# Moving the first two softmax heads ahead of v's eviction, and splitting that eviction between two engines, in a two-layer streaming encoder

## What is computed

```python
def even_mixer(h, P, ...):
    xa, ga, q, k, v = split(h @ w_in0)
    ya = rglru(xa, gates)[h] * gelu(ga)              # the recurrence
    s  = q @ k.T * DHB ** -0.5 + rel_bias            # 8 heads of 64
    yb = softmax(s) @ v
    return concat(ya, yb) @ w_out0
mod = silu(c) @ w_mod[l] + b_mod[l]                  # 1024 x 6144, for each layer
```

## Time and profile before

| | us |
|---|---|
| median of 3 runs | 1857.21 (1856.42 to 1857.47) |
| the profiled execution's own time | 1840.97 |
| its span, first to last instruction | 1839.2 |
| PE busy | 1715.2 (93%) |
| DVE busy | 860.9 (47%) |
| ACT busy | 278.8 (15%) |
| mean granted PE clock | 0.943 of full |

### The profile page before, as it was taken

One profiled execution on the slowest core, in us unless ns is written; L12 is line 12 of the kernel. 1 busy time (PEld: TensorE's weight loads), 2 busy tenths in 40 slices (PEclk: granted clock), 3 DMA queues, 4 the chain that ended last, 5 costly groups with the idle time before them and its releaser, 6 DMA issues.

```text
span 1839.2 us, 25633 instructions
## 1 busy us (share of the span) xinstructions
PE 1715.2 (93%) x9272; PEld 982.1 (53%) x9272; DVE 860.9 (47%) x2514; ACT 278.8 (15%) x643; POOL 112.7 (6%) x115
## 2 busy tenths in 40 slices
PE   5999998999999999998999888879999999999996
PEld 2663466544444444345776788756544444444443
DVE  3205424455555455445662654334455555555445
ACT  2132412100011001003112122102101100010001
POOL 0000000100000000000000232100100000000000
PEclk9997869999999999998999799679999999999998
DMA  9966833879999999995331000014779999999993
GB/s 384 333 257 240 318 140 138 316 325 420 419 420 418 409 419 420 419 420 203 115 137 69 0 1 1 3 72 183 280 312 420 419 420 414 406 421 419 419 421 136
DMA packets 81235, 528.08 MB, mean 287 GB/s; under 512 B 13104, under 2 KB 13632, under 8 KB 20400
## 3 DMA queue, kind: packets, MB, share of 16 engines
q1 hardware_dynamic: 68256, 496.14, 66.4%
q0 software_dynamic: 9024, 20.03, 2.9%
q10 hardware_dynamic: 3824, 10.20, 1.6%
HBM read 533.04 MB, written 5.86 MB: 293 GB/s over the span
## 4 chain that ended last, share of the span: by engine, by line
PE 82%; DMA 10%; DVE 5%; issue 2%; ACT 1%; SPq 0%; POOL 0%; ACTq 0%; DVEq 0%; POOLq 0%
PE ps L662 20%; PE ps L462 14%; PE ps L706 11%; PE ps L689 10%; DMA arena<-in_wexp 4%; DMA ring<-in_wexp 4%; PE ps L425 3%; PE ps L646 3%; DVE arena L1247 2%; PE ps L434 2%; PE ps L609 1%; PE ps L909 1%; PE ps L912 1%; PE ps L442 1%; PE ps L531 1%
## 5 line engine op out<-in xcount | busy, mean ns | idle before, releaser
L1253 DVE SCALAR_TENSOR_TENSOR x<-ps,mod,x 128x256 f32<-128x256 f32 (+1 forms) x1024 | 329.1, 363 | 188.8 <-PE ps L706 119.0
L662 PE MATMUL ps<-arena 128*32 128x512 f32 (+2 forms) x1456 | 308.0, 606 | 8.2 <-DMA arena<-in_wexp 8.2
L706 PE MATMUL ps<-arena 128*128 128x288 f32 x960 | 264.9, 417 | 6.4 <-DVE x L1253 4.3
L706 PEld LDWEIGHTS ps<-arena 128*128 128x128 f32 x960 | 172.2, 189 | 139.3 <-issue 94.2
L662 PE MATMUL ps<-ring,arena 128*64 128x512 f32 (+1 forms) x976 | 211.4, 597 | 1.2 <-DMA arena<-in_wexp 1.2
L462 PE MATMUL ps<-h,ring 128*128 128x288 f32 x768 | 193.6, 414 | 2.1 <-ACT h L1009 2.1
L662 PEld LDWEIGHTS ps<-arena 128*32 128x32 f32 (+2 forms) x1456 | 92.4, 128 | 149.6 <-issue 149.1
L462 PEld LDWEIGHTS ps<-h,ring 128*128 128x128 f32 x768 | 148.3, 194 | 43.8 <-issue 3.0
L1247 DVE TENSOR_TENSOR arena<-ps,arena 128x256 f32<-128x256 f32 (+6 forms) x153 | 56.1, 373 | 213.2 <-issue 170.2
L689 PE MATMUL ps<-ring,arena 128*64 128x512 f32 (+2 forms) x624 | 135.5, 628 | 11.1 <-DMA ring<-in_wexp 11.1
L1561 DVE COPY arena<-ps 128x512 f32<-128x512 f32 x60 | 41.5, 691 | 174.0 <-PE ps L689 168.9
(11 more groups left out here) (270 smaller groups left out, 1670.0 us busy)
## 6 DMA issues: line engine op xcount, KB each, us to landing
arena<-in_wexp SPq DMA_DIRECT2D x210, 1024.0 KB, 23.3
ring<-in_wexp SPq DMA_DIRECT2D x180, 1024.0 KB, 23.0
ring<-in_wmod SPq DMA_DIRECT2D x48, 1024.0 KB, 7.3
ring<-in_win SPq DMA_DIRECT2D x26, 1024.0 KB, 5.1
ring<-in_wout SPq DMA_DIRECT2D x8, 1024.0 KB, 4.9
h_rows<-arena ACTq DMA_DIRECT2D x4, 512.0 KB, 2.6
x<-in_x ACTq DMA_DIRECT2D x1, 1152.0 KB, 16.3
out_y<-h SPq DMA_DIRECT2D x2, 576.0 KB, 2.8
```

The costliest lines, as they stand in the source:

```text
L662: last = mm(ps[2][w, :], xgT[:, r % 2, 4 * q + k, w], unit(("gu", l, s0 + i, q))[:, k * 512:(k + 1) * 512], start=(q == 0 and k == 0), sto ...
L706: mm(ps[ADD_BANKS[c]][:, 0:T], yb[:, r % 2, c * 128:(c + 1) * 128], onehot[:, r % 2, :], start=True, stop=True).then_inc(sem["add_ps"], 1)
L1253: return V.scalar_tensor_tensor(out=o, in0=a, scalar=s, in1=b, op0=op0, op1=op1)
```

## The change

The maxima of heads 0 and 1, the exponential of both, and the normalisation of head 0 now stand ahead of v's eviction. ACT evicts v's first tile (new semaphore `v_ev0`) and DVE the other two. PE's wait for v moves behind the scores of head 2 and the transpose of head 0. ACT's three stores of v stand where the exponential of head 1 stood. The closing steps of the recurrence are spread behind the normalisations of heads 0, 2 and 3 (`finish`). No instruction is added or dropped but the waits, and one copy changes its engine.

PE:

```diff
-            pe.wait_ge(sem["v_ev"], 1)
             for n, (j, hd) in enumerate(units):
...
                 last.then_inc(sem["pt_ps"], 1)
+                if n == 0:
+                    pe.wait_ge(sem["v_ev0"], 1)
+                    pe.wait_ge(sem["v_ev"], 1)
```

ACT:

```diff
             softmax_exp(0)
+            softmax_exp(1)
+            act.wait_ge(sem["v_ps"], 2)
+            A(vtm[:, 0, :], ps[4][:, :], ACT.Copy).then_inc(sem["v_ev0"], 1)
             for b in range(MOD_AHEAD // 2):
                 mod_rows(1, b, 3)
-            act.wait_ge(sem["v_ev"], 1)
-            for j, (t0, P) in enumerate(TILES):
-                act.dma_start(t["v"][t0:t0 + P, :], vtm[0:P, j, :]).then_inc(sem["st_mix"], 16)
             for n in range(24):
...
-                if n + 1 < 24:
-                    softmax_exp(n + 1)
+                if n:
+                    if n + 1 < 24:
+                        softmax_exp(n + 1)
+                else:
+                    act.wait_ge(sem["v_ev0"], 1)
+                    act.wait_ge(sem["v_ev"], 1)
+                    for i, (i0, R) in enumerate(TILES):
+                        act.dma_start(t["v"][i0:i0 + R, :], vtm[0:R, i, :]).then_inc(sem["st_mix"], 16)
```

DVE:

```diff
+            def finish(n):
+
+                if n == 0:
+                    L(V.tensor_copy(hst[:, :, 0:1], hh[:, :, NP_ - 1:NP_]))
+                    L(V.tensor_copy(hst[:, :, 1:2], hh[:, :, SEG + NS - 1:SEG + NS]), "hst")
+                elif n == 2:
+                    L(stt(ycat[:, 0:4, 0:NP_], hh[:, :, 0:NP_], 0.5, gaT[:, :, 0:NP_], ALU.mult, ALU.mult))
+                elif n == 3:
+                    L(stt(ycat[:, 0:4, NP_:T], hh[:, :, SEG:SEG + NS], 0.5, gaT[:, :, NP_:T], ALU.mult, ALU.mult), "ya")
+
             softmax_max(0)
-            dve.wait_ge(sem["v_ps"], 2)
-            for j, (t0, P) in enumerate(TILES):
-                L(V.tensor_copy(vtm[0:P, j, :], ps[4 + j][0:P, :]), "v_ev" if j == 2 else None)
...
+            softmax_max(1)
             for n in range(24):
                 P, nk = TILES[n // 8][1], (128, 256, T)[n // 8]
-                if n + 1 < 24:
+                if 0 < n < 23:
                     softmax_max(n + 1)
                 dve.wait_ge(sem["p_exp"], n + 1)
                 L(V.reciprocal(rsum[0:P, n % 2, :], rsum[0:P, n % 2, :]))
                 L(ts(s_sb[0:P, n % 2, 0:nk], s_sb[0:P, n % 2, 0:nk], rsum[0:P, n % 2, :], None, ALU.mult), "p_nrm")
+                if n == 0:
+                    dve.wait_ge(sem["v_ps"], 2)
+                    L(V.tensor_copy(vtm[:, 1, :], ps[5][:, :]))
+                    L(V.tensor_copy(vtm[0:NS, 2, :], ps[6][0:NS, :]), "v_ev")
+                finish(n)
```

More of the change, by code:

```diff
@@ L156 @@
 SEMS = """ld_small ld_rest ld_att ld_state st_mix st_small st_out w_used mod_row mod_t cond lamn lame lam sq ss rms hs h
- proj_ps proj_ev v_ps v_ev pad conv hst gate_ps gate_e lru_a lru_w ya
+ proj_ps proj_ev v_ps v_ev v_ev0 pad conv hst gate_ps gate_e lru_a lru_w ya
  s_ps s_sm p_exp p_nrm pt_ps pt_sb pv_ps pv_sb out_ps out_x
@@ L1364, in softmax_max @@
                 L(ts(mx[0:P, n % 2, 1:2], mx[0:P, n % 2, 0:1], -1.0, None, ALU.mult), "s_sm")
-            softmax_max(0)
-            dve.wait_ge(sem["v_ps"], 2)
-            for j, (t0, P) in enumerate(TILES):
-                L(V.tensor_copy(vtm[0:P, j, :], ps[4 + j][0:P, :]), "v_ev" if j == 2 else None)
[L1370 to L1373, removed]
+            def finish(n):
[6 more added lines that the diff above has]
+                    L(stt(ycat[:, 0:4, NP_:T], hh[:, :, SEG:SEG + NS], 0.5, gaT[:, :, NP_:T], ALU.mult, ALU.mult), "ya")
+            softmax_max(0)
+            softmax_max(1)
             for n in range(24):
                 P, nk = TILES[n // 8][1], (128, 256, T)[n // 8]
-                if n + 1 < 24:
+                if 0 < n < 23:
                     softmax_max(n + 1)
```

## The result

The changed kernel takes 1827.36 us (median of 4 runs, 1825.03 to 1830.47), the kernel before 1856.82 us (4 runs, 1847.8 to 1857.47). The ratio is 0.9838, 95% interval 0.9814 to 0.9861: 29.5 us less, where 14.9 were forecast. 1827.36 lies 0.6 us under the range's lower end. Four executions that lasted 2047 to 6092 us, three of the kernel before and one of the changed kernel, are left out of every range and median here. The profiled execution of the changed kernel takes 1830.47 us with a span of 1828.7, so between the two profiled executions the gain is only 10.5 us. Both facts need explaining.

A forecast was written before the change was run, and what follows sets the result against it. PE, busy 93% of the span, was taken as the bound, with a wait and half clock in layer 0's attention. 3.5 + 11.35 = 14.9 us off 1857.21 gave 1842.3 us, range 1828 to 1854.

The forecast's parts named there:

- The wait: PE before the first tile's loop: head 0's normalisation moved earlier starts the `w_mod` unit at 158.69, not 162.20; 3.5 us gained.
- the covers: Margins at PE's first waits: v's eviction done by 158.3, PE there at 158.69; head 0's probabilities by 160.4, wanted at 160.60.
- The closing steps: Recurrence's end on DVE, two large steps of 1.55 us now behind heads 2 and 3: costed at nothing, 0.3 us as bound.
- The clock in the first tile: Layer 0's attention, 162.20 to 187.78 us: full clock kept, 14.23 us in place of 25.58, gaining 11.35 us.
- The loads: Weight units for the first tile: 2.65 us each at 396 GB/s against 2.56 per head; 0.7 us behind over eight heads, costing nothing.
- The first rival: Clock falls again within the first tile: 1848.0 to 1853.7 us, taken as 1849; chance 0.18.
- the sum's last: Sum's closing step: the runs' median lies 16.24 us above the profiled 1840.97 us, carried as a constant.
- the clock's term: The sum's 11.35 us for full clock through the first tile, bounds 11.0 to 11.9 us.
- The slower rival: Clock falls at the first tile's end, second tile at half clock: loses 25.6 against 14.9 gained, 1867.9 us; chance 0.05.
- the third tile: Forecast keeps half clock from 222 to 256.93; rival keeps full clock, up to 15.5 us more, 1826.8 at best; chance 0.17.
- The shift to the end: Behind the attention: experts' stream starts earlier by what the attention gains; nothing is given back, output projection at about 242.

The follow-up runs named there:

- the filled gap: Kernel before plus six unread matmuls on PE between head 2's scores and head 0's transpose, DVE and ACT order untouched: 1831.9 us, ratio 0.9856.
- the second profile: Kernel before, unedited, profiled once more: 1857.92 us, span 1856.1 us; output projection starts at 271.06 us.

## Why the prediction was wrong, by its own steps

- **The wait** was right. 3.5 us were forecast, and the unit of `w_mod` starts 162.20 - 158.75 = 3.45 us earlier. Two of the covers held with room: the eviction, and the copy of head 0's probabilities, which ended at 159.71 where 160.4 was its bound. The closing steps were hidden as costed, and the 1.23 us piece at 163.28 delays nothing. A small pause of 0.27 us, not in the sum, stands ahead of the first unit, for the row of `mod`. One reading was wrong without harm: rows of the trace do show both engines evicting at once, DVE until 156.26 + 2.13 = 158.39 and ACT from 157.96.
- **The clock in the first tile** was right in direction, and right in size against the profiled execution: 5.07 us for two heads (5.11 forecast), and the projection 15.7 us earlier (14.9 forecast). The loads kept up, at 419 GB/s over 162 to 170 us where 396 were counted on. The first rival, a new fall in the first tile, did not happen; neither did the slower one. One reading behind the first rival was loose: the fall at 222 was said to agree with idle moments between groups, but its row shows PE busy for 2.00 of 2.00 us, so it does not show such moments.
- **The step that failed** is the sum's last: "The median of the runs is 16.24 us above it; the trace does not explain that, and I carry it as a constant." It was no constant. In both profiled executions the time exceeds the span by 1.77 us alone. Nearly all of the 16 us are half-clock time of the second tile, caused by the same idle time and removed with it, as the filled gap shows. So the clock's term was mis-sized: 11.35 us by the profiled execution, but 271.06 - 241.19 - 3.45 = 26.4 us by the ordinary one. Together with the wait that makes 29.9 us, and 29.5 were measured.
- **The slower rival** had named the very stretch, the second tile at half clock, with a price of up to 25.6 us. It was put on the changed kernel alone. Going by the times, the kernel before had it in most of its executions, which its spread of 1840.97 to 1857.47 should have suggested. Two readings set against the rivals rested on the one profile: that the first tile's heads bring the clock back at 187, and that the second tile's wide matmuls hold it at 1.00. In the second profile the same heads and the same matmuls ran at 0.50 until about 221.
- **The range** allowed more gain only through the third tile (kept clock, down to 1826.8). That tile stayed at half clock, so the range's low end came close to the time by luck, for a wrong reason. (Half of the third tile kept would by its own figures be 1842.3 - 7.75 = 1834.6, not 1833.)
- **The shift to the end** was right but for layer 1's delta rule. From its input to its output projection it lasted 357.6 us in the profile before and 362.0 in the one after, at mean clocks of 0.88 and 0.86:

```profile
870.70:1228.30 357.60, 316.68 (x1910) 263.16 (x1908) 175.31 (x397) 63.60 (x146) 43.26 (x41) 0.88 0.12 45
```

```profile
855.80:1217.80 362.00, 321.29 (x1911) 266.33 (x1909) 175.47 (x397) 63.60 (x146) 42.78 (x41) 0.86 0.12 44
```

That is 4.4 of the 5.2 us by which the two profiles' gain, 10.5 us, falls short of the attention's 15.7. The stage is untouched by the change. Over all executions profiled it took 357.0 to 362.2 us, in edited and unedited kernels alike, so it seems to belong to where the clock's changes happen to fall; no run tested that. The prediction had allowed two to five microseconds for this.

## What to carry to other kernels

Where PE waits a few microseconds between light steps, price the clock behind the wait as well as the wait: here 3.5 us of idle time cost some 26 us more in a stretch that showed no idle time at all. When the median of the runs lies far from the profiled execution, profile the kernel again before calling the difference a constant, and look at where the clock returns. Matmuls that nobody reads are a cheap test of such a theory, and in a stretch of light work they can pay for themselves.

## What the runs showed of the hardware

- The fall at 160 us came in each of the three profiled executions that left PE idle there for 1.44 or some 3.4 us, and in none of those that left 0.57 us or less. The return differed by 34 us between two executions of one kernel: within 186 to 188, or within 220 to 222, with PE shown busy from 162 us on in both.
- The clock falls without any visible idle time where PE runs many small matmuls (third tile: 2.00 of 2.00 us busy over 220 to 222 in the earlier trace rows, then 0.50). With 18 extra matmuls of 288 columns laid between it stays at 1.00; with 13 it falls later and for some 7 us. The Trainium skill's page "TensorE: Matmul & The Clock Gate", Part 1, says that the slow state is the default and that activity releases it; the runs with 13 and 18 extra matmuls agree, with 1.00 over 206 to 220 us where the changed kernel has 0.58.
- DVE and ACT evicted neighbouring banks at the same time, in 0.69 and 0.60 us, as long as each took in the kernel before while the other stood idle.
